# Splitting ten GQA input tiles and both attention output projections into fp32r products

## The reference

```python
def _gqa_mixer(h, angles, ctx_k, ctx_v, w_in, q_norm, k_norm, w_out):
    proj = h @ w_in                       # 1024 x 1536: 8 query, 2 key, 2 value tiles
    q, k = _rms_norm(...), _rms_norm(...) # per head
    ...                                   # rotary positions for latent tokens
    o = _blocked_attention(q, k_all, v_all, GQA_HEAD_DIM ** -0.5)
    return o.reshape(B, N, nq) @ w_out, k, v
def _mla_mixer(...):
    ...
    return o.reshape(B, N, MLA_HEADS * MLA_V) @ w_out, ckv, krope
```

## Time and profile before

| | |
|---|---|
| median of three runs | 2134.77 us (2133.05 to 2138.92) |
| profiled execution, its own time | 2139.05 us |
| its span in the trace | 2137.2 us |
| PE busy | 2006.5 us, 94% |
| PEld busy | 1402.0 us, 66% |
| DVE busy | 1301.4 us, 61% |
| ACT busy | 1028.5 us, 48% |
| HBM read | 373.96 MB, 177 GB/s over the span |

### The profile page before, as it was taken

One profiled execution on the slowest core, in us unless ns is written; L12 is line 12 of the kernel. 1 busy time (PEld: TensorE's weight loads), 2 busy tenths in 40 slices (PEclk: granted clock), 3 DMA queues, 4 the chain that ended last, 5 costly groups with the idle time before them and its releaser, 6 DMA issues.

```text
span 2137.2 us, 44861 instructions
## 1 busy us (share of the span) xinstructions
PE 2006.5 (94%) x18880; PEld 1402.0 (66%) x18881; DVE 1301.4 (61%) x2497; ACT 1028.5 (48%) x1779; POOL 246.2 (12%) x363
## 2 busy tenths in 40 slices
PE   6999999899998999899899999999999999998996
PEld 4666666557876665677665656777566666656874
DVE  2666666438895341788722326888666666528896
ACT  3344444227774341677523315775544444316774
POOL 1432222110001000100010001000322232101000
PEclk9999999999999999999999999999999999999998
DMA  9244333247885244798622356897311121124890
GB/s 394 96 148 166 125 125 144 106 170 284 308 309 212 83 169 156 259 319 320 238 96 104 122 195 229 302 327 283 121 47 66 46 71 46 46 81 160 311 316 31
DMA packets 56909, 381.18 MB, mean 178 GB/s; under 512 B 6400, under 2 KB 10624, under 8 KB 12144
## 3 DMA queue, kind: packets, MB, share of 16 engines
q1 hardware_dynamic: 51696, 373.00, 48.5%
q10 hardware_dynamic: 4608, 4.20, 0.6%
q0 software_dynamic: 384, 0.89, 0.1%
HBM read 373.96 MB, written 4.10 MB: 177 GB/s over the span
## 4 chain that ended last, share of the span: by engine, by line
PE 84%; DVE 9%; ACT 4%; issue 2%; DMA 1%; SPq 0%; DVEq 0%; ACTq 0%
PE ps L854 15%; PE ps L1518 8%; PE ps L1522 7%; PE ps L1521 7%; PE ps L804 4%; PE ps L780 4%; PE ps L760 4%; PE ps L1307 3%; PE ps L995 3%; DVE e_wlo L2897 3%; PE ps L1552 2%; PE ps L1474 2%; PE ps L815 2%; PE ps L1407 2%; PE ps L1376 2%
## 5 line engine op out<-in xcount | busy, mean ns | idle before, releaser
L2897 DVE TENSOR_TENSOR e_wlo<-ring,e_whi 128x1024 fp32r<-128x1024 f32 x384 | 459.1, 1222 | 82.7 <-ACT e_whi L1759 79.3
L1759 ACT ACTIVATE e_whi<-ring 128x1024 fp32r<-128x1024 f32 x384 | 402.9, 1060 | 107.6 <-PE ps L1522 103.0
L854 PE MATMUL ps<-bufh,ring 128*128 128x384 f32 x1024 | 389.1, 501 | 2.2 <-ACT scratch L1759 0.9
L854 PEld LDWEIGHTS ps<-bufh,ring 128*128 128x128 f32 x1024 | 175.5, 190 | 93.8 <-issue 17.3
L1518 PE MATMUL ps<-e_whi,e_hs 128*128 128x512 f32 x512 | 210.6, 411 | 21.1 <-DVE e_wlo L2897 17.8
L1759 ACT ACTIVATE scratch<-ps 128x384 f32<-128x384 f32 (+6 forms) x311 | 109.1, 368 | 212.9 <-PE ps L854 53.7
L1522 PE MATMUL ps<-e_whi,e_hs 128*128 128x512 f32 x512 | 200.5, 392 | 0.0
L1521 PE MATMUL ps<-e_wlo,e_hs 128*128 128x512 f32 x512 | 199.9, 390 | 0.0
L3046 POOL TENSOR_SCALAR bufx<-bufo,x_gb 128x384 f32<-128x384 f32 x56 | 37.6, 686 | 1046.3 <-DVE bufo L2334 1046.3
L1518 PEld LDWEIGHTS ps<-e_whi,e_hs 128*128 128x128 f32 x512 | 96.0, 188 | 62.9 <-ACT e_whi L1759 40.8
L2429 DVE SCALAR_TENSOR_TENSOR scratch<-scratch,par 128x386 f32<-128x386 f32 x192 | 128.3, 668 | 4.8
(11 more groups left out here) (315 smaller groups left out, 3423.7 us busy)
## 6 DMA issues: line engine op xcount, KB each, us to landing
ring<-in_moe SPq DMA_DIRECT2D x192, 1024.0 KB, 4.9
ring<-in_w_ada SPq DMA_DIRECT2D x96, 1024.0 KB, 5.4
ring<-in_gdn_w_in SPq DMA_DIRECT2D x32, 1024.0 KB, 6.8
ring<-in_gdn_w_out SPq DMA_DIRECT2D x8, 1024.0 KB, 4.9
ring<-in_gqa_w_in SPq DMA_DIRECT2D x6, 1024.0 KB, 5.0
ring<-in_gqa_w_out SPq DMA_DIRECT2D x4, 1024.0 KB, 7.2
ring<-in_mla_w_out SPq DMA_DIRECT2D x4, 1024.0 KB, 8.0
ring<-in_mla_w_in SPq DMA_DIRECT2D x3, 1024.0 KB, 5.7
```

The lines of the kernel that those rows point to most:

```text
L854: last = mm(ps[:, head_bank(n, m), 0:T], w[:, m % 2, kt, :], bufh[:, kt, :], start=(kt == 0), stop=(kt == KT - 1))
L1759: return op(out, in_, ACT.Copy, **kw)
L2897: return tt_(e_wlo[:, b, :], w, e_whi[:, b, :].bitcast(F32), ALU.subtract)
```

## The change

Tiles 2 to 11 of the GQA input projection (`pos`, ten of twelve) and all tiles of the GQA and the MLA output projection are computed as three fp32r products per step instead of one fp32 product. For this

- ScalarE rounds each weight tile from the ring into one of two buffers in `scratch` (`weights_high`), VectorE writes the remainder beside it (`weights_low`); both wait until the tile two places back is done. PE waits for both parts before a tile's first product (`triple_tile`), and frees the ring's unit there.
- ScalarE rounds h tile by tile (`in_hi`), VectorE writes the remainder over h in place once tiles 0 and 1, which stay fp32, have been computed.
- The heads' outputs are split too: heads 0 to 4 from `bufo` in turns 16 to 22 (`LATE_HEADS`), heads 5 to 7 straight from PSUM.
- The weight parts of output tiles 0 and 1 are made behind turns 17 and 18 of the sweep (`SPLIT_AT`), those of tiles 2 to 7 on ScalarE as buffers come free and on VectorE inside `residual`.
- PE computes seven heads' part of output tile 0 ahead of the last value product.
- ScalarE's semaphore `chain_a` is dropped.

The diff, cut to its core:

```diff
+LATE_HEADS = {16: 0, 17: 1, 19: 2, 20: 3, 22: 4}
+HI_ORDER = (0, 1, 5, 2, 3, 6, 4, 7)
+SPLIT_AT = {17: 0, 18: 1}
+TILE = KT * P
+IN_TRIPLES = 10
+OUT_TRIPLES = {1: IN_TRIPLES, 2: IN_TRIPLES + KT}
...
+        def triple_done(eng, n):
+            if n < IN_TRIPLES:
+                eng.wait_ge(tile_mm, tiles_at["in", 1] + 1 + n + 1)
+            else:
+                l = 1 if n < OUT_TRIPLES[2] else 2
+                eng.wait_ge(tile_mm, tiles_at["out", l] + n - OUT_TRIPLES[l] + 1)
...
# PE
-            def project_out(l, ready, n_ready):
-                pe.wait_ge(ready, n_ready)
-
-                project(l, "out", 0, KT, bufo, (0, 1),
-                        lambda t: pe.wait_ge(r_ready, KT * l + t - 1) if t >= 2 else None)
+            def triple_tile(l, n, bank, steps, low, first, last, frees):
+                w = t_parts[l][:, n % 2, :, :].rearrange("p s (k c) -> p s k c", k=KT)
+                if first:
+                    pe.wait_ge(t_hi, n + 1)
+                    pe.wait_ge(t_lo, n + 1)
+                for i, (kt, part, of_low, ready) in enumerate(steps):
+                    if ready:
+                        ready()
+                    mul = mm(ps[:, bank, 0:T], w[:, part, kt, :], (low if of_low else t_high[l])[:, kt, :],
+                             start=(first and i == 0), stop=(last and i == len(steps) - 1))
+                    if first and i == 0 and frees:
+                        mul.then_inc(ring_free, 1)
+                if last:
+                    mul.then_inc(tile_mm, 1)
...
+            def project_out(l):
+                for t in range(1, KT):
+                    if t >= 2:
+                        pe.wait_ge(r_ready, KT * l + t - 1)
+                    out_tile(l, t, range(KT), True, True)
...
                     if qt == 0 and h:
                         pe.wait_ge(oh_ev, h0 + h)
+                        if h > 5:
+                            low_head(pe, l, h - 1)
...
+                pe.wait_ge(exp_done, a0 + H * TT - 1)
+                out_tile(l, 0, HI_ORDER[:-1], True, False)
                 value(H * TT - 1)
-                project_out(l, oh_ev, h0 + H)
+                out_tile(l, 0, HI_ORDER[-1:], False, True)
+                project_out(l)
...
+                if pos >= 2:
+                    if pos == 2:
+                        pe.wait_ge(in_hi, KT)
+                        steps = [(kt, part, False, None) for part in range(2) for kt in range(KT)]
+                        steps += [(kt, 0, True, lambda kt=kt: pe.wait_ge(in_lo, kt + 1)) for kt in range(KT)]
+                    else:
+                        steps = three_of(range(k0, k1))
+                    triple_tile(l, pos - 2, bank, steps, h_low, k0 == 0, k1 == KT, pos % 2)
+                    return
...
# ScalarE
-                a.step(op(g_tmp[:, 0, :, :], cum[:, 0, :, :], ACT.Exp))
+                op(g_tmp[:, 0, :, :], cum[:, 0, :, :], ACT.Exp)
...
+            def weights_high(l, n, u, half):
+                if n >= 2 and n - 2 not in (OUT_TRIPLES[2] - 2, OUT_TRIPLES[2] - 1):
+                    triple_done(act, n - 2)
+                landed(act, u)
+                copy(t_parts[l][:, n % 2, 0, :], unit(u)[:, TILE * half:TILE * half + TILE]).then_inc(t_hi, 1)
...
                     if n in JOINTS:
                         joint(JOINTS[n])
+                    if n in LATE_HEADS:
+                        act.wait_ge(oh_ev, h0 + LATE_HEADS[n] + 1)
+                        copy(t_high[l][:, LATE_HEADS[n], :], bufo[:, LATE_HEADS[n], :]).then_inc(in_hi, 1)
+                    if n in SPLIT_AT:
+                        out_high(l, SPLIT_AT[n])
                 head_out(H - 1)
+                for t in range(2, KT):
+                    out_high(l, t)
...
             def gqa_taken(pos):
...
+                if 2 <= pos < IN_TRIPLES:
+                    in_high(l_gqa, pos + 2)
...
# VectorE
-            def residual(l, src, rbuf, ready):
+            def residual(l, src, rbuf, ready, after=None):
 
                 dve.wait_ge(ax_ready, 2 * l + 1)
                 for k in range(KT):
                     ready(k)
+                    if after:
+                        after(k)
...
+            def weights_low(l, n, u, half):
+                dve.wait_ge(t_hi, n + 1)
+                parts = t_parts[l][:, n % 2, :, :]
+                tt_(parts[:, 1, :], unit(u)[:, TILE * half:TILE * half + TILE], parts[:, 0, :].bitcast(F32),
+                    ALU.subtract).then_inc(t_lo, 1)
...
                     if n + 1 < H * TT:
                         weights(n + 1)
                     joint(n)
-                residual(l, lambda k: ps[:, k % 2, :], bufh, lambda k: tile_done(dve, "out", l, k))
+                    if n in LATE_HEADS:
+                        head_low(l, LATE_HEADS[n], bufo[:, LATE_HEADS[n], :])
+                    if n >= 6 * TT and n % TT == 0:
+                        head_low(l, n // TT - 1, ps[:, 4, 0:T])
+                    if n in SPLIT_AT:
+                        out_low(l, SPLIT_AT[n])
+                head_low(l, H - 1, ps[:, 4, 0:T])
+                residual(l, lambda k: ps[:, k % 2, :], bufh, lambda k: triple_done(dve, OUT_TRIPLES[l] + k),
+                         lambda k: out_low(l, k + 1) if 1 <= k < KT - 1 else None)
...
             def gqa(l):
+                in_low(l, 2)
+                used(dve, mix_unit(l, "w", 0))
+                for k in range(KT):
+                    dve.wait_ge(in_hi, k + 1)
+                    tt_(h_low[:, k, :], bufh[:, k, :], t_high[l][:, k, :].bitcast(F32), ALU.subtract).then_inc(in_lo, 1)
+                in_low(l, 3)
                 for kv in range(2):
...
+                    in_low(l, 4 + kv)
...
                 gqa_pair_ready(0)
+                in_low(l, 6)
                 def joint(n):
                     if n in JOINTS:
                         gqa_pair_ready(JOINTS[n])
+                    if n in GQA_PIECES and GQA_PIECES[n][2] == KT and GQA_PIECES[n][0] < IN_TRIPLES:
+                        in_low(l, GQA_PIECES[n][0] + 2)
+                in_low(l, 7)
```

More of the change, by code:

```diff
@@ L402, in trunk @@
             pass
+        with nc.sbuf_tensor("bufo_r", [P, KT, T], F32R) as bufo_r, \
+                nc.sbuf_tensor("scratch_r", [P, SCRATCH], F32R) as scratch_r:
+            pass
         ps = ctx.enter_context(nc.psum_tensor("ps", [P, 8, 512], F32))
@@ L493, in trunk @@
         q_root = c(H * TT)
+        q_free = c.at
         c = Carve()
@@ L538, in trunk @@
         tile_mm, y_out = sems("tile_mm y_out")
-        chain_v, chain_a, chain_p = sems("chain_v chain_a chain_p")
+        chain_v, chain_p = sems("chain_v chain_p")
         (ab_mm, sp_in, ab_act, sp_ln, g_ready, cum_mm, cum_ready) = sems(
@@ L577, in trunk @@
             tiles_at["in", l] = n_tiles
-            n_tiles += {"gdn": 2 * H, "gqa": 6, "mla": 3}[kind]
+            n_tiles += {"gdn": 2 * H, "gqa": 1 + IN_TRIPLES, "mla": 3}[kind]
             tiles_at["out", l] = n_tiles
-            n_tiles += 4
+            n_tiles += 4 if kind == "gdn" else KT
         att_at = {1: 0, 2: H * TT}
@@ L782, in project, with three_of, out_tile @@
                     last.then_inc(tile_mm if t % 2 == 0 else ring_free, 1)
-            def project_out(l, ready, n_ready):
-                pe.wait_ge(ready, n_ready)
-                project(l, "out", 0, KT, bufo, (0, 1),
-                        lambda t: pe.wait_ge(r_ready, KT * l + t - 1) if t >= 2 else None)
+            def triple_tile(l, n, bank, steps, low, first, last, frees):
[12 more added lines that the diff above has]
+                    mul.then_inc(tile_mm, 1)
+            def three_of(kts):
+                return [(kt, part, of_low, None) for kt in kts for part, of_low in ((0, False), (0, True), (1, False))]
+            def out_tile(l, t, heads, first, last):
+                steps = three_of(heads)
+                if t == 0:
+                    for i, h in enumerate(heads):
+                        steps[3 * i] = (h, 0, False, lambda h=h: high_head(pe, l, h))
+                        steps[3 * i + 1] = (h, 0, True, lambda h=h: low_head(pe, l, h))
+                triple_tile(l, OUT_TRIPLES[l] + t, t % 2, steps, bufo_r, first, last, t % 2)
+            def project_out(l):
[3 more added lines that the diff above has]
+                    out_tile(l, t, range(KT), True, True)
             def out_part(l, t, k0, k1):
@@ L1755, in _ @@
             op = nc.scalar.activation
-            a = Chain(act, chain_a)
             def copy(out, in_, **kw):
@@ L2004, in scan, with out_high @@
                     state_in(l, n)
+            def weights_high(l, n, u, half):
[3 more added lines that the diff above has]
+                copy(t_parts[l][:, n % 2, 0, :], unit(u)[:, TILE * half:TILE * half + TILE]).then_inc(t_hi, 1)
+            def out_high(l, t):
+                if l == 2 and t < 2:
+                    act.wait_ge(cache_out, 16 * 4)
+                weights_high(l, OUT_TRIPLES[l] + t, unit_at["out", l] + t // 2, t % 2)
```

(32 more changed lines are left out.)

24 lines of the change are left out of this document (20 added, 4 removed).

## The result

The changed kernel took 2160.12 us, the median of four runs (2154.68 to 2169.14), beside 2133.91 for the kernel before in the same comparison: a ratio of 1.0118, 95% interval 1.0094 to 1.0143, so 25 us or 1.2% slower. The forecast had the sign, and several of its places, but said 2149.5 with 2158.0 as the upper end: the cost was under-sized.

The account below looks back on a forecast made before the run. PE was taken as the bound, gaining only where it need not wait for its feeders. Terms 2.7 + 5.9 + 5.8 + 0 + 0.3 = +14.7 us on the 2134.77 median gave 2149.5, range 2139 to 2158.

Parts of the forecast that it names:

- PE's price: Split tiles on PE: 24 products at 176 ns, 4.22 us against 5.19, saving 0.96 each, 25 us gross over 26.
- rival D: Three fp32r products no faster than one fp32 with weights from scratch; output tiles lose 0.96 each, 2165; chance 0.03.
- Item 1: Output projections: low part of tile k+1 waits for tile k, exposing 1.47 us at six boundaries per layer; +2.7 for both.
- Item 2, GQA: Last turns of the GQA sweep: output tiles' parts hold up the queues, delaying turns 19 and 20; +5.9 us.
- Item 2, MLA: Last turns of the MLA sweep: both queues wait for the weights' landing, turn 19 +3.05 late; +5.8 us in all.
- rival B: New idle stretches before tile 6's piece and at turns 19 and 20 also slow PE's clock; +5, 2154.5; chance 0.20.
- the likeliest case: The forecast's own case, the summed items without a rival: 2149.5 us, range 2143 to 2156, chance 0.60.
- Item 3: Input projection tiles 2 to 6: 2.75 us won, then lost to PE's wait for tile 6's low part; taken as 0.
- Item 4: GQA sweep pieces, rest of tile 6 to tile 11: -5.4 gained, 5.7 lost, including about 1.8 at each of two joints; +0.3.
- item 2 at 7 + 7: High-end assumption for the last turns of both sweeps, 7 us each, used with rival B to reach 2158.
- Rival A: Stalls in the sweeps fall into VectorE's idle time, so not slower: -3.8, 2131; turn 19 decides; chance 0.14.
- Rival C: Parts always ready, 25 us gained and all else hidden: 2110; needs low part k+1 before tile k's end; chance 0.03.

Follow-up runs that it names:

- the run with the filler: Changed kernel plus unused fp32 identity products on PE in the waits around turn 19 of both sweeps; 1.0093 against the kernel before.
- the repeat: The changed kernel unaltered, measured again in a later comparison; 1.0107 (1.0079 to 1.0135) against the kernel before.
- that line moved and three others: Changed kernel: output lows ahead of `ready(k)`, output tiles 0/1 parts later, tile 6's low before rotation, tiles 9/11 lows behind turns 5/12; 0.9936, 2121.79 us.
- the run with the latest parts: Against the fastest kernel (0.9936): output tiles 0 and 1 get high parts behind turns 20 and 21, low parts behind 22 and 23; 0.9948.

## Why the prediction was right in sign and wrong in size

- **PE's price.** Right: the pitch of the split tiles without a wait is 4.22 us, 24 products of 176 ns; rival D is out. The 162.5 ns did not come about, so the row was the one to take. They are an estimate by a formula of the Trainium skill ("TensorE: Matmul & The Clock Gate", Back-to-back issue gap), which that section gives for isolated products, saying that in a stream of weight loads and products both set the spacing. The difference on the 16 output tiles, 384 products x 13.75 ns, is 5.3 us, not 4.8.
- **Item 1, the output tiles.** The mechanism was right to the line. The size was off: +4.8 by the stages for both layers, against +2.7. The failing term is "end of tile to VectorE 0.11": that row counts from the start of another matmul behind the tile. An fp32r tile's last product starts at 828.11, a next one would start at 828.29, and VectorE starts at 828.49, 0.20 later. Then 1.23, 0.14 to PE, and the first product behind a wait takes 0.25 instead of 0.18: each boundary exposes 1.65 us (5.86 less 4.22), not 1.47. Twelve times, +2.1.
- **Item 2, GQA.** +5.2 against +5.9: turn 19 at +2.0 and turn 20 at +4.8 behind turn 18, where +2.25 and +4.95 stood, and the heads' lows less than 0.9. The landing did not matter here; the two queues did.
- **Item 2, MLA.** The step that failed most. The waits were right: the run with the filler has +5.9 for them, and turn 19 came 3.7 late instead of 3.05 because the unit landed 8.2 us after its issue instead of 7.4; in the four other profiles with this wait turn 19 came 2.9 to 3.4 late, so 3.05 was right and the 3.7 is the landing of one execution. What was left out of the sum is the clock: 10.2 us at half, +2.4 to +3.2. The forecast had it as rival B at 0.20, as something beside the waits; here it is a consequence of them, and it belonged in the likeliest case. By the Trainium skill, "TensorE: Matmul & The Clock Gate", section "Why this matters for your kernels", idle gaps between bursts of products put the clock back to half. The trace agrees at turn 19 of the MLA sweep, where the clock fell inside a wait of 3.67 us (2.84 in the shortest case); in the GQA sweep it fell behind two shorter waits, 1.85 and 1.86, and the gaps of 1.41 us between the output tiles left it at 1.00, as forecast.
- **Item 3, input tiles 2 to 6.** The wait ahead of tile 6 was 3.40 us (forecast 3.6), tile 4 lost 0.97 (1.1). But PE was through with the rotation at 716.87 where its next piece stood at 718.46: 1.6 us won by then, not 2.75. Tiles 0 to 2 won 0.2 us instead of 0.96: tiles 0 and 1 took 10.96 us instead of 10.69, and tile 2's last eight products went at the pace of h's low parts on VectorE, which began only with tile 1 done (no wait was forecast). The piece ran at half clock. Together with item 4 it is +2.1 in the profile against +0.3, and that excess is the clock: 10.2 us at half from 717 on, where before has 6.8. With 6.8 us the split input side measured -0.3 and -0.5, so the sizes of items 3 and 4 were right within 1 us.
- **Item 4, the joints.** Right: 5.47 to 7.25 us, 1.8 each, and both came back when the low part was moved.
- **The sum.** By stages: 14.7 + 2.1 (item 1, the hand-over) + 1.8 (items 3 and 4, the longer half clock) + 2.9 (MLA tail, the clock and a late landing) - 0.7 (GQA tail) = 20.8, the difference of the profiles. The high end of the range was 23.2 above the base, more than these stages hold; item 2 at 7 + 7 = 14 is even what the tails measured, 13.9. So the stages alone would have stayed inside. The medians differ by more: 26 us in the first comparison, 23 by the ratio of the repeat, and those 2 to 5 us were not found in a stage. Part of it is the base: 2134.77, like the 2133.91 of the comparison, lies 2.5 to 4.7 us below the four later medians of the same kernel (2137.28 to 2138.64). That the time came out above 2158 is thus the under-sized sum on top of a low base; the rest stays open.
- **Rival A** is out: turn 19 came late in both sweeps. **Rival C** (25 us gained) asked for the low part ahead of the tile's end. With that line moved and three others the kernel gains 14 us by its ratio, 17.9 by its profile. The missing 7 of 25 us stand in the GQA stage up to turn 18, where 5.1 of 9.6 us were won, and in the tails, which keep 2.6 and 0.2. The run with the latest parts shows for the GQA tail that the copies cost their time wherever they stand; for the stage ahead of it this was not tried.

## What to carry to other kernels

When a step is split into parts that other engines make, ask of each part where in its engine's in-order queue it stands, not how busy the engine is: behind the wait for tile k, the part for tile k+1 is late by its whole length every time. Put the two halves of a hand-over (ScalarE's copy, VectorE's subtraction) in different turns, behind the loads' landing and behind whatever is in the chain. And where a forecast has PE idle between pieces of small work for as long as here (3 us once, or 1.9 us twice), look for a stretch at half clock behind it in a like stage and price it as part of the wait. Compare two profiles' stages only at equal clock.

## What the runs showed of the hardware

- The half clock follows the idle stretch here, not the load: fp32 products of 128 columns without a use, put into the gap, kept it at 1.00, and the stretch between turns 19 and 21 of the MLA sweep was 2.4 to 3.2 us shorter for them. Without them the fall lasted 10.2 us behind waits of 2.8 to 3.7 us and 3.4 us behind a pair of 1.85 and 1.86, in five profiles of five. But long waits are not the only way to it: the kernel before falls to half at 718.5 for 3.4 us behind small products with gaps of 0.19 and 0.42 us, and six gaps of 1.41 us between runs of 24 large products brought no fall.
- The clock goes with much of the scatter between runs. Over 29 runs of the kernel before, the mean granted clock lay between 0.973 and 0.982, and the span fell by 15 us per 0.01 of it (correlation -0.86); in its three later sets of runs it was 9 to 15 us. Short stretches fall to half in one profile and not in the next; a profile's stage should be compared only with the clock of that stretch beside it (tile 0 to turn 18 took 113.73 us without such a stretch and 115.66 with 6.8 us of it, PE's operations being the same).
- An fp32r product's weight load is 188 ns long by the records and the products follow each other every 176 ns, 14 more than half an fp32 record of the same width. Whether the load sets that pitch was not tried.
